# A head's value product is issued one slot later, together with the next head's transposes and scores, in both softmax attentions of a two-block layer

## What is computed

```python
# first block, 16 heads: q, k of 128 + 64 columns, v of 128, causal
s = q @ k.T * scale; s = where(causal, s, -1e30)
o = softmax(s) @ v                    # later: (o * silu(z_b)) @ w_b
# second block, 8 heads of 128
s = q @ k.T - slope * dist            # three dilated windows, merged into one table
o = softmax(s) @ v
```

## Time and profile before

| what | us |
|---|---|
| median of 3 runs (2128.98 to 2129.07) | 2128.99 |
| the profiled execution, its own time | 2128.22 |
| its span, first to last instruction | 2126.4 |
| TensorE busy in the span | 2102.9 (99%) |
| VectorE busy | 1413.0 (66%) |
| ScalarE busy | 1069.3 (50%) |
| GpSimd busy | 37.8 (2%) |

### The profile page before, as it was taken

How to read it: one execution, slowest core, us unless ns; L and a number is a source line. 1 busy time by engine, 2 the same in 40 slices (tenths; PEclk the granted TensorE clock), 3 DMA queues, 4 the chain that set the end, 5 groups by cost and what they waited for, 6 DMA issues and landing times.

```text
span 2126.4 us, 24876 instructions
## 1 busy us (share of the span) xinstructions
PE 2102.9 (99%) x10088; PEld 1756.4 (83%) x10088; DVE 1413.0 (66%) x1813; ACT 1069.3 (50%) x1374; POOL 37.8 (2%) x49
## 2 busy tenths in 40 slices
PE   8999999999999999999999999999999999999998
PEld 7888888888888877788888888888888888888886
DVE  5877788875555775556554455456786787687675
ACT  6445555555444674454454444354544454454443
POOL 0000000000000020000000000000000000000000
PEclk9999999999999999999999999999999999999999
DMA  7455555564465534365755542445555455555553
GB/s 270 178 190 188 196 198 205 191 244 178 174 226 198 188 139 158 122 235 198 292 179 184 191 158 100 158 179 206 190 198 197 178 198 202 192 185 213 181 195 119
DMA packets 56562, 402.59 MB, mean 189 GB/s; under 512 B 6240, under 2 KB 6496, under 8 KB 9216
## 3 DMA queue, kind: packets, MB, share of 16 engines
q1 hardware_dynamic: 53648, 380.67, 49.5%
q0 software_dynamic: 2656, 19.81, 2.4%
q10 hardware_dynamic: 144, 0.52, 0.1%
HBM read 392.59 MB, written 8.39 MB: 189 GB/s over the span
## 4 chain that ended last, share of the span: by engine, by line
PE 95%; ACT 2%; DVE 1%; issue 1%; DMA 0%; SPq 0%; POOLq 0%; POOL 0%; DVEq 0%; ACTq 0%
PE proj L574 15%; PE proj L576 15%; PE proj L575 15%; PE proj L1029 11%; PE proj L1032 6%; PE proj L679 4%; PE proj L681 4%; PE proj L680 4%; PE tbank L679 2%; PE tbank L680 2%; PE tbank L681 2%; PE tbank L547 2%; PE bank_a L679 1%; PE bank_a L681 1%; PE bank_a L680 1%; PE bank_b L679 1%
## 5 line engine op out<-in xcount | busy, mean ns | idle before, releaser
L1646 DVE TENSOR_TENSOR w_lo<-raw,w_hi 128x1024 fp32r<-128x1024 f32 x714 | 849.9, 1203 | 584.6 <-ACT w_hi L1134 576.7
L1134 ACT ACTIVATE w_hi<-raw 128x1024 fp32r<-128x1024 f32 x714 | 739.8, 1043 | 881.8 <-PE proj L576 503.8
L574 PE MATMUL proj<-w_hi,a_both 128*128 128x512 f32 x1280 | 512.2, 400 | 0.0
L576 PE MATMUL proj<-w_hi,a_both 128*128 128x512 f32 x1280 | 499.8, 390 | 0.0
L575 PE MATMUL proj<-w_lo,a_both 128*128 128x512 f32 x1280 | 498.4, 389 | 0.0
L576 PEld LDWEIGHTS proj<-w_hi,a_both 128*128 128x128 f32 x1280 | 240.2, 188 | 51.7
L574 PEld LDWEIGHTS proj<-w_hi,a_both 128*128 128x128 f32 x1280 | 240.5, 188 | 51.1 <-issue 4.3
L575 PEld LDWEIGHTS proj<-w_lo,a_both 128*128 128x128 f32 x1280 | 240.7, 188 | 47.5
L1029 PE MATMUL proj<-a_both,w_hi 128*128 128x512 f32 x1024 | 256.5, 392 | 0.3 <-DVE a_both L1689 0.3
L1029 PEld LDWEIGHTS proj<-a_both,w_hi 128*128 128x128 f32 x1024 | 184.4, 189 | 33.7 <-DVE a_both L1689 0.5
L1032 PEld LDWEIGHTS proj<-a_both,w_lo 128*128 128x128 f32 x1024 | 139.7, 190 | 10.0
(11 more groups left out here) (449 smaller groups left out, 2651.8 us busy)
## 6 DMA issues: line engine op xcount, KB each, us to landing
raw<-stream SPq DMA_DIRECT2D x359, 1024.0 KB, 4.8
nat<-x SPq DMA_DIRECT2D x4, 512.0 KB, 8.0
z_store<-z POOLq DMA_DIRECT2D x1, 2048.0 KB, 8.9
ga_store<-z POOLq DMA_DIRECT2D x1, 2048.0 KB, 12.5
gb_store<-z POOLq DMA_DIRECT2D x4, 512.0 KB, 7.6
yb<-z_store POOLq DMA_DIRECT2D x4, 512.0 KB, 8.5
ga<-ga_store POOLq DMA_DIRECT2D x1, 2048.0 KB, 8.0
gb<-gb_store POOLq DMA_DIRECT2D x1, 2048.0 KB, 14.4
```

What stands on the lines that cost most here:

```text
L574: nc.tensor.matmul(banks[t][:, :], ah, wh, start=first, stop=False)
L576: last = nc.tensor.matmul(banks[t][:, :], al, wh, start=False, stop=end)
L1134: A((w_hi_end if extra else w_hi)[:, piece.n % RING, 0:width], src, ACT.Copy).then_inc(w_rounded, 1)
L1646: V.tensor_tensor(lo[:, s, 0:width], src, hi[:, s, 0:width].bitcast(f32), SUB).then_inc(w_rest, 1)
```

## The change

The value product of head h - 1 is issued at the start of the even slot of head h, ahead of its transposes and the scores of head h + 1. The odd slots hold no work of TensorE's for the heads any more, except the last one, which has the product of the last head. VectorE finishes head h - 1 in the odd slot of head h, and in the last odd slot the last two heads. The row sums `den` have four buffers in place of two.

```diff
--- before.py
+++ after.py
@@ -289,7 +289,7 @@
         inv_k = little("inv_k", [P, TT, 4])
         nmax = little("nmax", [P, 2, TT])
         nb = little("nb", [P, 2, TT])
-        den = little("den", [P, 2, TT])
+        den = little("den", [P, 4, TT])
         rden = little("rden", [P, TT])
         ss2 = little("ss2", [P, TT, 4])
         inv2 = little("inv2", [P, TT])
@@ -851,15 +851,17 @@
             def heads_b(n):
 
                 h, odd = divmod(n, 2)
-                if odd and h >= 0:
-                    if h == 0:
+                if not odd:
+                    if h == 1:
                         pe.wait_ge(proj_read, 2 * 45)
-                    values_b(h, t_of[h])
-                if not odd:
+                    if h >= 1:
+                        values_b(h - 1, t_of[h - 1])
                     if h >= 0:
                         t_of[h] = probs_b(h)
                     if h + 1 < H_B:
                         scores_b(h + 1)
+                elif h == H_B - 1:
+                    values_b(h, t_of[h])
 
             for c, name in enumerate(LATENT):
                 def slot(j, c=c):
@@ -929,15 +931,17 @@
             def heads_2(n):
 
                 h, odd = divmod(n, 2)
-                if odd and h >= 0:
-                    if h == 0:
+                if not odd:
+                    if h == 1:
                         pe.wait_ge(proj_read, 2 * (45 + 12 + 6))
-                    values_2(h, t_of[h])
-                if not odd:
+                    if h >= 1:
+                        values_2(h - 1, t_of[h - 1])
                     if h >= 0:
                         t_of[h] = probs_2(h)
                     if h + 1 < H_2:
                         scores_2(h + 1)
+                elif h == H_2 - 1:
+                    values_2(h, t_of[h])
 
             project(a_hi, a_lo, slot=lambda j: heads_2(j - 8) if j >= 6 else None)
             y2_first = by_dve.n
@@ -1381,9 +1385,9 @@
                     act.wait_ge(b_ready, h + 1)
                     s = stg[:, h % 2, :]
                     A(s[:, 0:P], s[:, 0:P], ACT.Exp, bias=nb[:, h % 2, 0:1], scale=inv_q[:, 0, h:h + 1],
-                      accum_out=den[:, h % 2, 0:1])
+                      accum_out=den[:, h % 4, 0:1])
                     A(s[:, P:384], s[:, P:384], ACT.Exp, bias=nb[:, h % 2, 1:2], scale=inv_q[:, 1, h:h + 1],
-                      accum_out=den[:, h % 2, 1:2]).then_inc(p_ready, 1)
+                      accum_out=den[:, h % 4, 1:2]).then_inc(p_ready, 1)
 
             def squares(c):
 
@@ -1490,7 +1494,7 @@
                     s = stg[:, h % 2, :]
                     for t in range(TT):
                         last = A(s[:, t * TOK:(t + 1) * TOK], s[:, t * TOK:(t + 1) * TOK], ACT.Exp,
-                                 bias=nmax[:, h % 2, t:t + 1], accum_out=den[:, h % 2, t:t + 1])
+                                 bias=nmax[:, h % 2, t:t + 1], accum_out=den[:, h % 4, t:t + 1])
                     last.then_inc(p_ready, 1)
 
             for i in range(2):
@@ -2088,7 +2092,7 @@
             def finish_head(h, n, dst, gate):
 
                 dve.wait_ge(o_done, n + 1)
-                chain(V.reciprocal(rden[:, :], den[:, h % 2, :]))
+                chain(V.reciprocal(rden[:, :], den[:, h % 4, :]))
                 for t in range(TT):
                     o, b = dst[:, t, h * P:(h + 1) * P], bank_b[:, t * P:(t + 1) * P]
                     if gate:
@@ -2125,10 +2129,12 @@
                     if h % 4 == 0:
                         dve.wait_ge(pow_done, (14, 16, 17, 18)[h // 4])
                     V.tensor_tensor(nb[:, h % 2, :], nmax[:, h % 2, :], inv_q[:, :, h], MUL).then_inc(b_ready, 1)
-                elif h >= 0:
-                    if h % 4 == 0:
-                        dve.wait_ge(yb_in[h // 4], 16)
-                    finish_head(h, h, yb, True)
+                elif h >= 1:
+                    heads = (h - 1, h) if h == H_B - 1 else (h - 1,)
+                    for h in heads:
+                        if h % 4 == 0:
+                            dve.wait_ge(yb_in[h // 4], 16)
+                        finish_head(h, h, yb, True)
 
             for c in range(len(LATENT)):
                 def slot(j, c=c):
@@ -2225,8 +2231,9 @@
                     dve.wait_ge(s_read, n + 1)
                     V.tensor_reduce(nmax[:, h % 2, :], s.rearrange("p (t k) -> p t k", t=2), AX.X, MAX,
                                     negate=True).then_inc(b_ready, 1)
-                elif h >= 0:
-                    finish_head(h, H_B + h, y2, False)
+                elif h >= 1:
+                    for h in (h - 1, h) if h == H_2 - 1 else (h - 1,):
+                        finish_head(h, H_B + h, y2, False)
 
             for i in range(1, 6):
                 pieces(slot=(lambda j: heads_2(j - 8) if j >= 6 else None) if i == 5 else None)
```

## The result

The median is 2149.15 us (2148.11 to 2150.11, 4 runs) against 2128.98 before; the ratio is 1.0094, with a 95% interval from 1.0082 to 1.0107. The kernel became 20.2 us slower. The profiled execution took 2148.11 us, 19.9 more than that of before. The four times stand in two pairs, 2148.1 and 2148.2, and 2150.1 and 2150.1; the kernel before has no such pairs.

The account below looks back on a forecast made before the run. TensorE, busy in 99% of the span, was taken to bound the kernel. Waits of 11.5 us (first attention) and 5.5 (second), less 0.3 saved, gave 16.7 us more: 2145.5 us predicted, range 2142.0 to 2149.5.

Parts of the forecast that it names:

- the forecast: Both attentions: new waits per head and at the ends, no clock fall; 2145.5 us, own range 2142.5 to 2148, chance 0.76.
- the rival with a fall: Long waits in slots 31 and 15: clock falls in one or both, 2148.1 or 2150.7 us, chance 0.14.
- The product itself: Value products joined to the transposes: 22 of 24 save one change of matmul shape, 0.2 to 0.3 us gained.
- The wait that moves with it: bank_b in even slots: VectorE's finish ends at T + 3.24, TensorE arrives at T + 2.72, 0.52 us early.
- How many heads: Waits counted over both attentions, full, short and at the ends: 11.5 us in the first, 5.5 in the second.
- What a wait on VectorE adds: Each product's wait: 0.05 us for the signal, 0.11 for an uncovered weight load, 0.16 together; 0.68 per head.
- The ends: Last odd slots: slot 31 costs 3.4 us; slot 15 costs 2.2 after taking over the wait for uf.
- The clock: Two new idle stretches of 3.2 to 3.4 us: no fall assumed; 2.6 us per fall if one comes.
- no new wait: bank_b in each even slot: VectorE done by T + 2.72, only the saved shape change remains; 2128.7 us, chance 0.04.
- only the two ends wait: Rounding and rest pass 0.5 us shorter, so only slots 31 and 15 wait; 2134.3 us, chance 0.06.

Follow-up runs that it names:

- experiment 7: The change's TensorE order, but VectorE finishes head h-1 in the even slot of head h, the last head in the last odd slot: 2128.22 us.
- The dose: One extra 0.45 us VectorE instruction per finish, in the change (2160.28 us) and in the kernel before (2129.26 us).
- experiment 4: The change with its two long waits removed, plus the product's two semaphore waits exchanged so that o_read is written first: 2139.83 us.
- both halves: The change in the first attention alone, 2142.12 us, and in the second attention alone, 2136.34 us; the other attention as in the kernel before.
- the slow finish: The change with one more VectorE instruction of 0.45 us ahead of each reciprocal in finish_head: 2160.28 us.
- the long waits alone: The change with heads finished in the even slot, except the last two of each attention in the last odd slot: 2137.41 us.
- the last experiment: The change's TensorE order with VectorE's finish one slot earlier, in the even slot in which the product is issued: 2128.22 us.
- `first_only`: The change in the first attention alone, the second as in the kernel before: 2142.12 us.
- experiment 6: The change with heads finished in the even slot, except the last two of each attention in the last odd slot: 2137.41 us, median of five.

## Why the prediction was right, and where it was not

2145.5 was forecast and 2149.15 measured, slower as said, and for the mechanism named. But the case that came true is not the forecast, which had no fall of the clock, its own range of 2142.5 to 2148 and a chance of 0.76: all four times lie above 2148. It is the rival with a fall (2148.1 or 2150.7). The median lies inside the range only because its upper end, 2149.5, took in one fall, and because two of the four times were the lower ones; the other two, 2150.1, lie outside. That part is luck. Point by point:

- *The product itself*, 0.01 us gained in each of 22: the right sign, and with the profile of experiment 7 rather 0.02 to 0.04. Right and without weight.
- *The wait that moves with it*: right to the hundredth. VectorE's finish ends at T + 3.24 after the change too, and TensorE stands in front of bank_b. The dose shows that this is cause and not company: 0.45 us more in the finish, 0.45 more in each wait.
- *How many heads*: right. 11 and 5 full waits, three and one short ones, two long ones; with the dose all 22 are visible in the waits. The view of the change counts 12 and 6 instead of the 15 and seven that were announced, because the short ones leave hardly any idle time in it.
- *What a wait on VectorE adds*: mis-sized. Forecast 0.05 for the signal and 0.11 for the load. Measured 0.15 for the signal, because two semaphores are waited for and the late one came last in the program (experiment 4), and 0.30 - 0.22 = 0.08 for the load (821.32 to 821.62 against 0.22 between the product's next lines). That makes 0.67 + 0.08 = 0.75 in place of 0.68 in a full wait, some 1.5 us over all 22. The row that I took as nearest waits for one semaphore alone; the bounds of 0.52 and 0.8 held.
- *The ends*: 3.38 + 0.08 = 3.46 in slot 31, against 3.4. In slot 15 the wait for uf disappeared behind the new one, as said.
- *The clock*: this is the step that failed. "I take no fall" rested on the idle end of the kernel, where the clock outlasted a longer idle time. It fell in the first or second long wait, or in both, in every profile that has these waits (the change, both halves, the slow finish, and the long waits alone), and in none without them. In the profiled execution it cost (1.84 - 0.89) + (0.86 - 0.44) = 1.4 us in the product and the transposes and some 0.2 in the matmul behind them. The rival with its price of 2.6 for a fall had the mechanism and a price somewhat too high; 0.14 was too small a chance for it. The Trainium skill's warning about idle TensorE between bursts ("TensorE: Matmul & The Clock Gate", "HAM oscillation — how this bites in real kernels") agrees with these traces: the clock read 0.51 in 1325 to 1328, after the wait.

For the profiled execution the terms make 16.7 + 1.5 + 1.6 = 19.8 us; measured are 19.9. The upper pair of times, 2150.1, fits a second fall, but this is argued and not shown: no profile of the change has two, though that of the slow finish does. Against a plain count of falls, each half, which has only one long wait, had one execution about 1.5 us above its median too (2143.61 and 2137.96) with a mean clock of 0.997, where its others had 0.998. More time at the lower clock than in the profiled executions also comes with one long wait; where it lies, no trace shows.

Of the rivals, "no new wait" and "only the two ends wait" are ruled out by the waits view. The second of them assumed that the rounding passes would be shorter without a product beside them; they kept their 1.06 and 1.23 us.

## What to carry to other kernels

When a producer is moved one slot later and its consumer stays where it is, look for the buffer between them and count in slots who frees it and who takes it again: here two pieces of distance became one, and the one was 0.5 us too short in each head. An engine at 66% of the span can still be late in every slot; its latency after the common event (3.24 us after the piece) is what counts, not its load. If the freeing work can move along with the product, as in the last experiment, nothing is lost.

## What was not expected of the hardware

- A long wait costs twice: TensorE idle for 3.2 us by the waits view came out of it at 1.2 GHz in some executions, not in all (slot 31 of the change stayed at 1.00, slot 31 of `first_only` did not). Three matmuls of no use in each of the two gaps made the kernel 2.7 us faster.
- With two semaphores before a matmul, the one written first is the cheaper one to be late: 0.05 us from the end of VectorE's instruction to the start of the matmul, against 0.15 where the late one is written last.
- What stays open: the single execution of 4308.83 us, about twice the others, the 0.4 to 0.7 us in experiment 6, and which executions of the change had how many falls.
